# Attention heads: the product with V placed between the sixth and seventh block of a projection

## Chip, cores and metric

One core of a Trainium2 chip runs the whole kernel as one program. The metric is the device time in microseconds (us); the kernel before takes 2199.02 us (median of 3 runs, 2193.82 to 2200.7).

## What is computed

Three transformer layers on 512 positions of width 1024: a retention layer, a layer with chunked attention, and a hybrid layer, each with a feed-forward part. The change lies in the second layer, in its 16 attention heads of width 64:

```python
q, k, v = jnp.split(h @ w_in, 3, axis=-1)            # h: 512 x 1024
s = einsum('bqhd,bkhd->bhqk', qb, kb) * scale + bias # a chunk of 64 queries, a band of up to 576 keys
p = jax.nn.softmax(s, axis=-1)
o = einsum('bhqk,bkhd->bqhd', p, vb)                 # the product with V
return o @ w_out
```

All of it is in fp32. A weight or an activation is split into a high and a low part (`w_hi`, `w_lo`, `x_hi`, `x_lo`), and three matmuls (high by high, high by low, low by high) stand for one.

## The kernel before

The weights come as a stream of 362 units of 512 KB through a ring of four buffers. For each unit SyncE issues the load, ScalarE (ACT) makes the high part (L978), VectorE (DVE) the low part (L1422), three units ahead of use, and TensorE (PE) uses it in a projection (`proj`): eight blocks of three matmuls with 512 columns (L508, L509, L510) that add up in bank 0 or 1 of PSUM. The order of the work on every engine is written out by hand, and semaphores tie the engines together.

The attention heads run as steps s = -1 to 16. In step s, TensorE works for three heads:

- `turn`: it transposes the probabilities of head s-1 into banks 5, 6 and 7 (ten transposes, L729). It waits until GpSimd (POOL) has normalised the probabilities (L2097). The last two transposes write bank 7, and before them it waits on the semaphore `att.o`, which the sum of the head before raises.
- `proj`: the projection of the q or the k tile of a later pair of heads, in steps -1 to 12. Steps 13 to 16 have `two_tiles` in its place: one unit of the output projection, in two halves of 12 matmuls.
- `weigh`: the product with V for head s-1, eight matmuls into bank 7 (L742, L744). It waits for `turned_lo`, the low parts of the transposed probabilities.
- `scores`: q by k for head s+1, eight matmuls (L708, L709), in steps up to 14. It waits for the parts of q and k, and for the `maxima` of head s.

The low part of V lies beside the high part in the stationary operand, so that the halves of bank 7 (64 partitions each) have to be added: ACT copies one half into the pair's tile (`o_part`, L1180), and DVE adds the other (`o_sum`, L1712), which raises `att.o`.

Steps alternate by `head_par`. The text calls a step with `head_par` 0 an even-head step (s = 1, 3, 5, 7, 9, 11, 13, 15) and one with `head_par` 1 an odd-head step (s = 2, 4, ..., 16). The queues of ACT and DVE in a step of the kernel before, in order:

- ACT, even-head: high part of V (`value_hi`, L1195), high parts of the transposed probabilities (`turned_his`, L1164), weight split (L978), four exponentials (L1156), `q_hi` (L1169), two `k_hi` (L1175), `o_part` (L1180).
- ACT, odd-head: the same without L1195; `q_hi` waits here for the q and k tile that DVE reads out of this step's projection (`qk_tile`, L1686), and from step 6 on `out_hi` (L1185) stands between `k_hi` and `o_part`.
- DVE, even-head: `maxima` of head s (L1659, L1663), low part of V (L1730), `turned_los` (L1674), weight split (L1422), `inverse` (L1679), `q_lo` (L1693), `k_lo` (L1700), `qk_tile` (L1686), `o_sum` (L1712).
- DVE, odd-head: the same without L1730, but `qk_tile` stands ahead of `q_lo` and `k_lo`, and `out_lo` (L1719) behind them, ahead of `o_sum`.
- In steps 13 to 16 DVE adds the two halves of `two_tiles` to `h` (L1472) in place of `qk_tile`; only step 13 has `q_hi`, `k_hi`, `q_lo`, `k_lo`, and steps 13 to 15 have `out_hi` and `out_lo`.
- POOL: it adds a mask to the next head's bias (L2110), normalises head s (four instructions, L2097) as soon as `inverse` is done, and loads a bias tile (L2105).

Of the kernel before, what the change touches and what calls it, by code (L numbers as in the profile page):

```python
# [46 lines left out]
HEAD, WINDOW = 64, 128  # L47
# [147 lines left out]
def build(nc, stream, x_t, cols, wf, f_bias, sinks, rel_pad, rel_2, c_rope, c_decay, c_sq, c_tri, c_sel,  # L195
# [3 lines left out]
    with ExitStack() as ctx:  # L199
# [80 lines left out]
        xl_ready = sem("xl_ready")  # L280
# [68 lines left out]
        att = Heads("att")  # L349
# [78 lines left out]
        def pair_tile(pair, a=0, b=P):  # L428

            if not pair.a:  # L430
                return arena[a:b, (9 + pair.b) * S:(10 + pair.b) * S]
            return arena[a:b, bass.ds((pair * S + 9 * S).val(), S)]
# [68 lines left out]
        def _(pe):  # L501
# [16 lines left out]
            def proj(src=xs, n=KT, first=None, hooks={}, bank=None):  # L518


                slot = at.u % RING
                wait(pe, lo_ready, at.u + 1)
                rotating = bank is None
                if rotating:
                    bank = banks[at.t % 2]

                    wait(pe, tile_read, at.t - 1)
                for k in range(n):
                    if k in hooks:
                        hooks[k]()  # L530
                    if first:
                        for s, base in first:
                            wait(pe, s, lin(base) + (k + 1))
                    m = mm3(bank[:, :], w_at(slot, k * P, k * P + P), src(k), k == 0, k == n - 1)
                m.then_inc(products_done, 1)
                at.step(1, 1 if rotating else 0)
# [50 lines left out]
            def two_tiles(src, first=None):  # L587

                slot = at.u % RING
                wait(pe, lo_ready, at.u + 1)  # L590
                for c in range(2):
                    wait(pe, tile_read, at.t - 1)
                    for k in range(4):
                        if first and c == 0:
                            wait(pe, first[0], first[1] + (k + 1))
                        m = mm3(banks[at.t % 2][:, :], w_at(slot, (4 * c + k) * P, (4 * c + k + 1) * P),
                                src(k), k == 0, k == 3)
                    m.then_inc(products_done, 1)
                    at.pe, at.t = at.pe + 1, at.t + 1
                at.u = at.u + 1  # L600
# [132 lines left out]
            def weigh(sm, hd, values, kind):  # L733


                window = kind == "window"
                ta, tw = (CT_AT, CT_W) if window else (T_AT, T_W)
                wait(pe, sm.turned_lo, hd * 4 + 4)
                wait(pe, sm.o, hd)
                for j in range(TT):  # L740
                    dst = banks[7][:, j * P:j * P + tw[j]]
                    pe.matmul(dst, values(j), pt_h[:, ta[j]:ta[j] + tw[j]], start=j == 0, stop=False,  # L742
                              skip_group_check=True)
                    m = pe.matmul(dst, values(j), pt_l[:, ta[j]:ta[j] + tw[j]], start=False, stop=j == TT - 1,  # L744
                                  skip_group_check=True)
                m.then_inc(sm.pv, 1)


            def staged(half):
                return lambda j: vs[:, j, half * P:half * P + P]  # L750
# [4 lines left out]
            def att_step(s, par, unit=True, late=True, early=True, half=None):  # L755


                head_par = par
                if late:
                    turn(att, s - 1, head_par, "chunk")  # L760
                if unit:
                    proj()
                if half is not None:

                    two_tiles(attended, (xl_ready, 24) if half == 0 else None)
                if late:
                    if head_par == 0:

                        wait(pe, stage_lo, (s + 1) // 2)
                    weigh(att, s - 1, staged(head_par), "chunk")  # L770
                if early:

                    wait(pe, att.qk_lo, s * 2 + 4)
                    wait(pe, att.biased, (s + 1) * 4)
                    if s.b == -1:

                        pe.wait_ge(masks_ready, 1)
                        pe.wait_ge(squares_landed, 16)
                        pe.wait_ge(att_v, 8)
                        pe.wait_ge(zeroed, 2)  # L780
                    scores(att, s + 1, head_par, "chunk")
# [178 lines left out]
        def _(act):  # L960
            hold = holder(xh_ready)
# [189 lines left out]
            def exps(sm, hd, par, window=False):  # L1151

                hold(act, (sm.negmax, hd + 1))
                for t in range(TT):
                    a, w = (CP_AT[t], CP_W[t]) if window else (P_AT[t], P_W[t])
                    act.activation(pf[par][:, a:a + w], pf[par][:, a:a + w], ACT.Exp, bias=nm[par][:, t:t + 1],  # L1156
                                   accum_out=sums[par][:, t:t + 1]).then_inc(sm.exp, 1)
# [19 lines left out]
            def o_part(sm, dst, half):  # L1177

                lo = HEAD * half
                act.activation(dst, banks[7][HEAD - lo:2 * HEAD - lo, :], ACT.Copy).then_inc(sm.o_part, 1)  # L1180
# [7 lines left out]
            def att_step(s, head_par, unit=False, late=True, early=True, pair=None, half=False, ended=None,  # L1188
                         sets=True):

                if late:
                    if head_par == 0:

                        hold(act, (att.pv, s - 1))
                        act.activation(value_hi(vs), two_heads(pair_tile(pair)), ACT.Copy).then_inc(stage_hi, 1)  # L1195
                    turned_his(att, s - 1)
                if unit:
                    split()
                    at.step()
                if half:  # L1200
                    split()
                    at.step(2, 2)
                if early:
                    exps(att, s, 1 - head_par)
                if sets:
                    if head_par:
                        wait(act, tile_read, at.t)
                    q_hi(att, 1 - head_par)
                    k_hi(att, 1 - head_par)
                if ended is not None:  # L1210
                    out_hi(ended)
                if late:
                    lo = HEAD * head_par
                    hold(act, (att.pv, s))
                    o_part(att, pair_tile(pair, lo, lo + HEAD), head_par)

            root(2)
            keep_rms(2)
# [186 lines left out]
        def _(dve):  # L1405
# [271 lines left out]
            def inverse(sm, hd, par):  # L1677
                wait(dve, sm.exp, hd * 4 + 4)
                dve.reciprocal(rinv[par], sums[par]).then_inc(sm.rinv, 1)  # L1679
# [41 lines left out]
            def att_step(s, head_par, unit=False, late=True, early=True, pair=None, half=None, ended=None,  # L1721
                         sets=True):

                if early:
                    hd = s
                    maxima(att, hd, 1 - head_par, (bias_masked, hd + 1), "rel")
                if late:
                    if head_par == 0:
                        wait(dve, stage_hi, (s + 1) // 2)
                        dve.tensor_tensor(value_lo(vs), two_heads(pair_tile(pair)), f32(value_hi(vs)),  # L1730
                                          ALU.subtract).then_inc(stage_lo, 1)
                    turned_los(att, s - 1)
                if unit or half is not None:
                    split()
                if early:
                    inverse(att, s, 1 - head_par)
                if sets and not head_par:
                    q_lo(att, 1, s * 3 + 6)
                    k_lo(att, 1, s * 3 + 6)
                if half is not None:  # L1740
                    at.u = at.u + 1
                    for c in range(2):
                        at.pe, at.t = at.pe + 1, at.t + 1
                        add_tile(2 * half + c)
                if unit:
                    at.step()
                    qk_tile(att, head_par, s * 2 + (6 - 2 * head_par))
                if sets and head_par:
                    q_lo(att, 0, s * 3 + 6)
                    k_lo(att, 0, s * 3 + 6)  # L1750
                if ended is not None:
                    out_lo(ended)
                if late:
                    lo = HEAD * head_par
                    hold(dve, (att.o_part, s))
                    o_sum(att, pair_tile(pair, lo, lo + HEAD), head_par)

            def first_pair(sm, n):
                for k in range(2):
# [579 lines left out]
```

## Time and profile before

| | |
|---|---|
| time of the profiled execution | 2198.44 us |
| its span | 2196.7 us |
| TensorE busy | 2127.8 us (97% of the span) |
| VectorE busy | 1239.8 us (56%) |
| ScalarE busy | 850.9 us (39%) |
| GpSimd busy | 270.8 us (12%) |
| mean granted TensorE clock | 0.988 of full speed |

The profile is of one execution. A matmul's row shows its start and its modelled length; matmuls overlap, so a busy TensorE has one 512-column matmul start every 0.23 us while each row says 0.39 us. A view's "idle before" is the time that the engine stood still before an instruction, with what ended it. The attention steps with the product with V lie between 879 and 1037 us of the span.

### The profile page before, as it was taken

How to read it: one execution, taken by the hardware profiler on the slowest of the kernel's cores; microseconds unless marked ns; L12 is line 12 of the kernel's file. 1: busy time of each engine (PE TensorE's matmuls, PEld its weight loads, DVE VectorE, ACT ScalarE, POOL GpSimd, SP SyncE). 2: the span in 40 equal slices, each digit the busy share in tenths (PEclk: the TensorE clock that was granted, in tenths of full speed). 3: DMA queues.
4: the chain of work that ended last, by engine and by line, in shares of the span. 5: the costliest groups of instructions: out<-in, count | busy, mean ns of one | idle time of the engine just before them, and what ended most of it. 6: DMA issues, size and time to landing. Idle time of an engine off the chain costs nothing.

```text
span 2196.7 us, 27184 instructions
## 1 busy us (share of the span) xinstructions
PE 2127.8 (97%) x9700; PEld 1752.2 (80%) x9700; DVE 1239.8 (56%) x1822; ACT 850.9 (39%) x1358; POOL 270.8 (12%) x312
## 2 busy tenths in 40 slices
PE   7899999899999999999999999999999999999997
PEld 5788888788888888777888888867887888888886
DVE  5264646464544543887645445556765456656674
ACT  4243333342222233776422222437662234333342
POOL 4122222310000010332100000302310010000001
PEclk9999999999999999999999999999999999999999
DMA  7532323123333233222333333321223222333332
GB/s 184 113 100 76 101 72 95 57 87 96 96 95 99 93 98 104 77 75 73 92 97 96 95 96 95 101 82 53 73 73 95 94 93 92 106 105 115 96 108 94
DMA packets 58124, 205.51 MB, mean 94 GB/s; under 512 B 7061, under 2 KB 7205, under 8 KB 58048
## 3 DMA queue, kind: packets, MB, share of 16 engines
q1 hardware_dynamic: 52704, 189.82, 27.7%
q0 software_dynamic: 3760, 11.92, 2.9%
q10 hardware_dynamic: 1584, 2.75, 0.3%
q8 instruction: 49, 0.80, 0.1%
q14 instruction: 27, 0.22, 0.0%
HBM read 198.43 MB, written 6.03 MB: 93 GB/s over the span
## 4 chain that ended last, share of the span: by engine, by line
PE 87%; DVE 5%; ACT 3%; issue 2%; POOL 1%; DMA 1%; ACTq 0%; DVEq 0%; POOLq 0%; SPq 0%
PE bank L508 28%; PE bank L510 27%; PE bank L509 27%; DMA raw<-in_stream 1%; PE bank L729 1%; DVE w_lo L1422 1%; POOL arena L2097 1%; ACT w_hi L978 1%; PE bank L744 1%; ACT arena L1156 0%; PE bank L708 0%; PE bank L742 0%; DVE arena_r L1674 0%; DVE h L1472 0%; ACT arena_r L1175 0%
## 5 line engine op out<-in xcount | busy, mean ns | idle before, releaser
L1422 DVE TENSOR_TENSOR w_lo<-raw,w_hi 128x1024 fp32r<-128x1024 f32 x358 | 465.1, 1300 | 288.5 <-ACT w_hi L978 288.5
L508 PE MATMUL bank<-x_hi,w_hi 128*128 128x512 f32 x1552 | 617.9, 398 | 7.3 <-DVE x_lo L1428 4.4
L510 PE MATMUL bank<-x_hi,w_lo 128*128 128x512 f32 x1552 | 607.4, 391 | 0.0
L509 PE MATMUL bank<-x_lo,w_hi 128*128 128x512 f32 x1552 | 607.2, 391 | 0.0
L978 ACT ACTIVATE w_hi<-raw 128x1024 fp32r<-128x1024 f32 x358 | 376.0, 1053 | 417.8 <-PE bank L510 394.0
L508 PE MATMUL bank<-arena_r,w_hi 128*128 128x512 f32 x1008 | 395.2, 392 | 13.6 <-POOL arena_r L2060 7.0
L510 PE MATMUL bank<-arena_r,w_lo 128*128 128x512 f32 x1008 | 393.1, 390 | 0.0
L509 PE MATMUL bank<-arena_r,w_hi 128*128 128x512 f32 x1008 | 393.0, 390 | 0.0
L508 PEld LDWEIGHTS bank<-x_hi,w_hi 128*128 128x128 f32 x1552 | 293.6, 189 | 73.1 <-DVE x_lo L1428 6.3
L509 PEld LDWEIGHTS bank<-x_lo,w_hi 128*128 128x128 f32 x1552 | 293.6, 189 | 62.1 <-issue 3.1
L510 PEld LDWEIGHTS bank<-x_hi,w_lo 128*128 128x128 f32 x1552 | 293.1, 189 | 62.1
L508 PEld LDWEIGHTS bank<-arena_r,w_hi 128*128 128x128 f32 x1008 | 189.6, 188 | 60.2 <-issue 12.1
L1472 DVE TENSOR_TENSOR h<-bank,h 128x512 f32<-128x512 f32 x152 | 104.5, 689 | 224.2 <-PE bank L510 224.0
L510 PEld LDWEIGHTS bank<-arena_r,w_lo 128*128 128x128 f32 x1008 | 189.7, 188 | 39.8
L509 PEld LDWEIGHTS bank<-arena_r,w_hi 128*128 128x128 f32 x1008 | 189.8, 188 | 38.5
L1467 DVE TENSOR_TENSOR arena<-bank,rbc 128x512 f32<-128x512 f32 x125 | 86.3, 690 | 171.7 <-PE bank L510 164.2
L1133 ACT ACTIVATE arena_r<-arena 128x512 fp32r<-128x512 f32 x64 | 40.5, 633 | 247.3 <-DVE arena L1624 247.3
L2033 POOL TENSOR_TENSOR acc<-sq 128x512 f32<-128x512 f32 x6 | 8.3, 1386 | 860.2 <-ACT sq L990 509.1
L2097 POOL TENSOR_SCALAR arena<-arena,small 128x256 f32<-128x256 f32 (+3 forms) x128 | 77.2, 618 | 289.2 <-DVE small L1679 244.9
L508 PE MATMUL bank<-w_hi,x_hi 128*128 128x512 f32 x224 | 87.6, 391 | 0.9 <-ACT arena L1232 0.9
L510 PE MATMUL bank<-w_hi,x_lo 128*128 128x512 f32 x224 | 87.2, 389 | 0.0
L509 PE MATMUL bank<-w_lo,x_hi 128*128 128x512 f32 x224 | 87.2, 389 | 0.0
(215 smaller groups left out, 2012.7 us busy)
## 6 DMA issues: line engine op xcount, KB each, us to landing
raw<-in_stream SPq DMA_DIRECT2D x358, 512.0 KB, 3.5
arena<-in_rel_pad POOLq DMA_DIRECT2D x16, 256.0 KB, 2.9
bias_strips<-arena POOLq DMA_DIRECT2D x1, 3840.0 KB, 55.2
h<-in_x_t ACTq DMA_DIRECT2D x8, 256.0 KB, 6.5
out_t<-h SPq DMA_DIRECT2D x8, 256.0 KB, 2.1
arena<-in_c_decay POOLq DMA_DIRECT2D x4, 256.0 KB, 2.9
arena<-bias_strips POOLq DMA_DIRECT2D x4, 256.0 KB, 3.8
arena<-bias_strips POOLq DMA_DIRECT2D x8, 128.0 KB, 2.4
```

The source lines that it names most:

```text
L508: pe.matmul(dst, lh, rh, start=start, stop=False, **kw)
L509: pe.matmul(dst, lh, rl, start=False, stop=False, **kw)
L510: return pe.matmul(dst, ll, rh, start=False, stop=stop, **kw)
L729: m = pe.transpose(banks[b][:, o + (t - j) * P:o + (t - j) * P + P], pf[par][:, src:src + P], ident[:, :])
L744: m = pe.matmul(dst, values(j), pt_l[:, ta[j]:ta[j] + tw[j]], start=False, stop=j == TT - 1, skip_group_check=True)
L978: act.activation(w_hi[:, u % RING, :], raw[:, u % RING, :], ACT.Copy).then_inc(hi_ready, 1)
L1133: act.activation(uh[j], uf[j % 2], ACT.Copy).then_inc(u_hi, 1)
L1422: dve.tensor_tensor(w_lo[:, s, :], raw[:, s, :], f32(w_hi[:, s, :]), ALU.subtract).then_inc(lo_ready, 1)
L1467: return dve.tensor_tensor(dst, banks[(at.t - 1) % 2][:, :], rbc[:, :], ALU.mult)
L1472: dve.tensor_tensor(h[:, j, :], banks[(at.t - 1) % 2][:, :], h[:, j, :], ALU.add).then_inc(tile_read, 1)
L2033: pool.tensor_tensor(acc[:, :], sq[:, 0, :], sq[:, 1, :], ALU.add).then_inc(acc_sum, 1)
L2097: pool.tensor_scalar(pf[par][:, a:a + w], pf[par][:, a:a + w], rinv[par][:, t:t + 1], 1.0, ALU.mult, ALU.mult).then_inc(sm.probs, 1)
```

## The change

In steps 1 to 12 `weigh` is no longer issued behind the projection but inside it, ahead of its seventh block. ACT's `o_part` goes ahead of `q_hi`, `k_hi` and `out_hi` in all steps 1 to 16. DVE's `o_sum` goes, in steps 1 to 12, directly behind `inverse`, ahead of `q_lo`, `k_lo`, `qk_tile` and `out_lo`; in steps 13 to 16 it stays last. The count and the kinds of the instructions stay the same. The hybrid layer's heads keep their order.

```diff
 # tensor
                 if late:
                     turn(att, s - 1, head_par, "chunk")
-                if unit:
-                    proj()
-                if half is not None:
-
-                    two_tiles(attended, (xl_ready, 24) if half == 0 else None)
-                if late:
+                def weigh_last():
                     if head_par == 0:
 
                         wait(pe, stage_lo, (s + 1) // 2)
                     weigh(att, s - 1, staged(head_par), "chunk")
+
+                if unit:
+                    proj(hooks={6: weigh_last} if late else {})
+                if half is not None:
+
+                    two_tiles(attended, (xl_ready, 24) if half == 0 else None)
+                    weigh_last()
...
 # scalar
                 if early:
                     exps(att, s, 1 - head_par)
+                if late:
+                    lo = HEAD * head_par
+                    hold(act, (att.pv, s))
+                    o_part(att, pair_tile(pair, lo, lo + HEAD), head_par)
                 if sets:
...
                 if ended is not None:
                     out_hi(ended)
-                if late:
-                    lo = HEAD * head_par
-                    hold(act, (att.pv, s))
-                    o_part(att, pair_tile(pair, lo, lo + HEAD), head_par)
...
 # vector
+                def sum_last():
+                    lo = HEAD * head_par
+                    hold(dve, (att.o_part, s))
+                    o_sum(att, pair_tile(pair, lo, lo + HEAD), head_par)
+
...
                 if early:
                     inverse(att, s, 1 - head_par)
+                if late and half is None:
+                    sum_last()
                 if sets and not head_par:
...
                 if ended is not None:
                     out_lo(ended)
-                if late:
-                    lo = HEAD * head_par
-                    hold(dve, (att.o_part, s))
-                    o_sum(att, pair_tile(pair, lo, lo + HEAD), head_par)
+                if late and half is not None:
+                    sum_last()
```

## Rows read from the trace of the kernel before

**Rows 1.** The page: busy us of TensorE, its share of the span, instructions.

```profile
PE 2127.8 (97%) x9700; PEld 1752.2 (80%) x9700; DVE 1239.8 (56%) x1822; ACT 850.9 (39%) x1358; POOL 270.8 (12%) x312
```

**Rows 2.** Waits, 870 to 1040 us: total us, times, longest us.

```profile
PE bank L729 <- DVE arena L1712: 8.8, 7, 1.6
...
PE bank L729 <- POOL arena L2097: 2.1, 2, 1.4
```

**Rows 3.** Busy us by stretch, step 6 and the start of step 7, then on.

```profile
929.90:940.80 10.90, 9.31 (x52) 7.91 (x51) 8.19 (x19) 8.30 (x19) 3.46 (x7) 1.00 0.31 98
940.80:950.20 9.40, 9.33 (x51) 7.84 (x52) 8.44 (x23) 7.01 (x17) 3.52 (x6) 1.00 0.18 57
```

**Rows 4.** Timeline of TensorE, steps 6 and 7: start us, length us.

```profile
929.97 0.48 PE L508 MATMUL bank<-x_hi,w_hi 128*128 128x512 f32 x1
...
935.51 0.39 PE L742 MATMUL bank<-arena_r 128*128 128x512 f32 x1
...
936.72 0.27 PE L708 MATMUL bank<-arena_r 128*128 128x128 f32 x1
...
938.05 1.03 PE L729 MATMUL bank<-ident,arena 128*128 128x128 f32 x8
...
940.67 0.44 PE L729 MATMUL bank<-ident,arena 128*128 128x128 f32 x2 [1.58 <-DVE arena L1712]
...
946.44 0.39 PE L742 MATMUL bank<-arena_r 128*128 128x512 f32 x1
```

**Rows 5.** Timeline of ACT and DVE between step 6 and step 7.

```profile
935.71 0.69 DVE L1686 SCALAR_TENSOR_TENSOR arena<-bank,rbc 128x512 f32<-128x512 f32 x1 [0.56 <-PE bank L510]
...
937.09 1.29 ACT L1175 ACTIVATE arena_r<-arena 64x512 fp32r<-64x512 f32 x2
...
938.28 0.62 ACT L1185 ACTIVATE arena_r<-arena  x1
938.41 0.68 DVE L1700 TENSOR_TENSOR arena_r<-arena,arena_r 64x512 fp32r<-64x512 f32 x1 [0.56 <-ACT arena_r L1175]
938.93 0.59 ACT L1180 ACTIVATE arena<-bank 64x512 f32 x1
939.20 0.69 DVE L1719 TENSOR_TENSOR arena_r<-arena,arena_r  x1
...
939.93 0.69 DVE L1712 TENSOR_TENSOR arena<-bank,arena 64x512 f32 x1
...
940.65 0.29 DVE L1659 CUSTOM_DVE_ANT_0 arena<-bank,arena 128x128 f32<-128x128 f32 x1
...
943.23 1.68 DVE L1674 TENSOR_TENSOR arena_r<-bank,arena_r 128x512 fp32r<-128x512 f32 x4
```

**Rows 6.** Timeline of GpSimd: the normalising of steps 6 and 7.

```profile
935.25 2.06 POOL L2097 TENSOR_SCALAR arena<-arena,small 128x128 f32<-128x128 f32 x4 [2.93 <-DVE small L1679]
...
946.23 2.93 POOL L2097 TENSOR_SCALAR arena<-arena,small 128x128 f32<-128x128 f32 x4 [5.38 <-DVE small L1679]
```

**Rows 7.** Timeline, TensorE's weight loads: the transposes of step 2.

```profile
889.76 1.07 PEld L729 LDWEIGHTS bank<-ident,arena 128*128 128x128 f32 x10 [1.80 <-POOL arena L2097]
```

**Rows 8.** Timeline, steps 13 to 16.

```profile
1006.64 0.63 ACT L1169 ACTIVATE arena_r<-arena 64x512 fp32r<-64x512 f32 x1
...
1007.34 0.39 PE L742 MATMUL bank<-arena_r 128*128 128x512 f32 x1
...
1012.01 0.44 PE L729 MATMUL bank<-ident,arena 128*128 128x128 f32 x2 [0.85 <-DVE arena L1712]
...
1019.79 0.69 DVE L1712 TENSOR_TENSOR arena<-bank,arena 64x512 f32<-64x512 f32 x1 [0.53 <-ACT arena L1180]
...
1020.31 0.93 PE L729 MATMUL bank<-ident,arena 128*128 128x128 f32 x7
...
1028.91 0.68 DVE L1712 TENSOR_TENSOR arena<-bank,arena 64x512 f32<-64x512 f32 x1 [0.54 <-ACT arena L1180]
1028.99 1.31 PE L729 MATMUL bank<-ident,arena 128*128 128x128 f32 x10 [0.74 <-POOL arena L2097]
```

## The prediction

> **What bounds the kernel now.** I read the page first: TensorE is busy for 97% of the span [rows 1], so a change of order can save only where TensorE stands still. The view of waits over the attention steps says how much that is and where: 8.8 us in seven waits for bank 7, which `o_sum` (L1712) has to release, and 2.1 us in two waits for GpSimd's normalising [rows 2]. The stretches show the rhythm: a step from an odd head to the next even head takes 10.90 us with 9.31 us of TensorE in it, the next one 9.40 us with 9.33 [rows 3]. So the wait stands in every second step, ahead of the even heads. The timelines of TensorE and of the two vector engines in steps 6 and 7 then say what is late: TensorE has issued eight transposes at 938.05, and the last two only come at 940.67, 1.58 us late [rows 4]. `o_sum` ended at 940.62, because it stands last in a queue of `qk_tile` 935.71, `k_hi` 937.09, `out_hi` 938.28, `o_part` 938.93, `out_lo` 939.20 and itself 939.93 [rows 5]. `o_part` needed only the product with V, done near 936.9, two us earlier.
>
> **What the change removes.** All times below are in the clock of the trace. A projection takes 935.51 - 929.97 = 5.54 us, so its six first blocks take 4.16 and the last two 1.38. `weigh` takes 936.72 - 935.51 = 1.21, `scores` 938.05 - 936.72 = 1.33 [rows 4]. In step 6 `weigh` would be issued at 934.13 and over at about 935.5. `o_part` (0.59) and `o_sum` (0.69) follow [rows 5] and end at about 936.9; bank 7 is needed at 938.9. So this wait goes, all seven times: 8.8 us of gain if nothing takes its place.
>
> **What takes its place, steps 2 to 12.** Moving `weigh` ahead of two blocks delays the end of the projection by 1.21. `qk_tile` starts at 936.92 instead of 935.71, just behind the moved `o_sum`. From there the old queue runs, without `o_part` and `o_sum`: `qk_tile` to 937.61, `q_hi` to 938.27, the two `k_hi` (1.29) to 939.59, `k_lo` (0.68) to 940.30, `out_lo` (0.69, 0.1 of gap) to 941.06 [rows 5]. `maxima` of step 7 starts at 941.10, before at 940.65: later by 0.45, though a sum has left the queue. Behind `maxima` stand the low part of V and `turned_los`, which before ran from 943.23 to 944.91 [rows 5] and now ends at 945.36.
>
> TensorE, freed of its wait, starts the projection of step 7 at 939.12 and reaches the seventh block at 943.28. There it now meets `weigh`, which needs `turned_los`: it stands still for 2.1 us, inside the projection. Before, `weigh` came at 946.44 [rows 4], 1.5 us after its data, and hid this chain. Now it comes at 945.42, 1.0 us earlier, but 1.38 us of projection still lie behind it. 945.42 + 1.21 + 1.38 + 1.33 = 949.34 is the start of the next transposes; before it was 946.44 + 1.21 + 1.33 = 948.98 and a wait of 0.25 for GpSimd. The next projection starts at 950.41 against 950.28 (929.90 + 10.90 + 9.40 and the same 0.07 [rows 3]): +0.1 per pair of steps. So the removed wait comes back in full, in another place. The first two pairs have no `out_hi` and `out_lo` in the queue; I take 0 for them, and +0.1 for the next three, together +0.3.
>
> GpSimd is the other thing that the next step waits for. `inverse` stands behind the weight split, so its start moves from 946.23 to about 946.68. At 2.93 us, as before, it would end at 949.61 and add 0.3 more per pair, six times 1.6 in all at the worst; at 2.06, as in step 6 [rows 6], it is hidden. The 2.93 is there because `q_lo` and `k_lo` run at the same time. The change puts them behind `o_part`, so that at most `q_lo` meets its last instruction. I take half of the 0.87 and hence no wait. [...]
>
> In step 7 `q_hi` now waits for `o_part`, hence for the product. `k_lo` ends at 950.15, `qk_tile` at 950.84, and `maxima` of step 8 starts 1.0 us later than before; its `turned_los` ends at 954.4. Step 8 reaches its seventh block at 950.41 + 4.16 = 954.57. That hides it by 0.15 us and no more.
>
> **The first steps.** The transposes of step 2 waited 1.80 us for GpSimd [rows 7], so that placing `weigh` earlier gives nothing there; only less contention at GpSimd can, 0 to 0.87. I take -0.5.
>
> **Steps 13 to 16.** TensorE's order is the same, but ACT now puts `o_part` ahead of `q_hi`, `k_hi` and `out_hi`, while DVE still adds last. In step 13 `weigh` comes at about 1006.25 (before 1007.34, [rows 8], less the 1.0 gained by then), `o_part` ends at 1008.3, and `q_hi` starts then instead of at 1006.64 [rows 8]. `k_hi`, `k_lo`, both additions to `h`, `out_lo` and `o_sum` follow, as before in that order: bank 7 comes free at 1013.55, before at 1012.01 [rows 8]. **+1.5 us.** In steps 14 and 15 `out_hi` (0.62) and `out_lo` (0.69) ran before during `two_tiles`; now they stand between `o_part` and `o_sum`, +1.3. In step 14 `o_sum` ended at 1020.48 and bank 7 was needed at 1020.31 + 0.84 = 1021.15 [rows 8]: 0.7 was hidden, **+0.7**. In step 15 it ended at 1029.59 and was needed at 1029.85 [rows 8]: **+1.0**. Step 16 has no `out_hi`; +0.2 for what GpSimd and DVE drag behind. Together +3.4, the largest term of the sum.
>
> **Nothing else moves.** SyncE's loads and ACT's weight splits keep their place and lead of three units; the bias loads follow the normalising within half a microsecond; the hybrid layer is untouched. The clock reads 1.00 in both stretches, with waits of 1.6 us in them [rows 3]; a wait of 2.1 us is near that, and I count no change.
>
> **Sum.** -0.5 + 0.3 + 3.4 = +3.2 us on the profiled execution, 2198.44 to 2201.6. That execution lies 0.6 below the median of the runs, so 2202 for the median: +0.15%, less than what a measurement of this kernel tells from no change (0.3%, 6.6 us).
>
> **Rivals.**
>
> 1. *The gain arrives.* If `turned_los` were done when the seventh block is reached, the 8.8 us would stay and only steps 13 to 16 give back 3.4: 2194, -0.25%; without that loss too, 2190, -0.4%. For it speaks that ACT is idle in parts of the queue and the chain is worked out from single starts. Against it: the gap is 2.1 us, each of the DVE instructions in it is read off, and none of them leaves.
> A variant: TensorE could do the last two blocks during the new wait, 6 x 1.38 = 8.3 us. In the trace its projection did not start while two transposes waited for bank 7, though nothing held it [rows 4]. The Trainium skill, TensorE: Matmul & The Clock Gate, section "The mechanism", says that matmuls are "strict FIFO, no reordering"; by that rule, which speaks against the change, the trace agrees.
> 2. *Slower.* One mechanism: in even-head steps `q_hi` waits for the product, which pushes `qk_tile` and `maxima` of the next step by 1.0. Only 0.15 us hides it. If the queue there is longer than my sum (`k_lo` took 0.92 beside GpSimd, 0.68 alone), odd-head steps wait inside their projection too, and what they lose, the next even-head chain starts later by. The bound is that nothing hides `o_part` and `o_sum`, 0.59 + 0.69 - 0.15 = 1.1 us in each of six pairs: 6.8 + 3.2 = +10, 2209, +0.45%. It decides from 0.6 us per pair, where the whole is over 6.6.
> 3. *No effect.* Another engine ends the wait for bank 7 first (the probabilities of the even heads, say), so that steps 2 to 12 stay and only the tail is lost: 2202. The rows name L1712 seven times; it comes to the same number.
>
> **Chances and range.** My forecast, the waits trade places and the tail loses a little: 0.60. The gain arrives: 0.13, about two thirds of it beyond 0.3%. Slower by the q and k split: 0.20, nearly all beyond. No effect: 0.07. A few hundredths of the forecast's own spread, its terms ranging from -0.9 - 0.3 + 2 = +0.8 to 1.6 + 0.3 + 3.4 + 1.5 = +6.8, lie beyond the bound as well. So faster 0.10, same 0.67, slower 0.23. The likeliest case alone spans 2199 to 2207; the range that takes in part of both rivals is 2194 to 2208.
>
> **What the profile after would show.** Right: the waits of L729 for L1712 are gone in steps 2 to 12; L742 waits about 2 us for L1674 in even-head steps, between two blocks; a pair of steps still takes 20.3 to 20.5 us; L729 waits longer for L1712 in steps 14 to 16 (about 2.3, 0.7 and 1.0). Wrong: L742 waits in odd-head steps too, or hardly at all; pairs shorter than 19.5 or longer than 20.9; GpSimd's four instructions still take 2.9 and end the wait.

## The result, and the profile after

The changed kernel takes 2203.67 us (median of 16 runs) against 2196.94 us before. The two medians lie 6.7 us apart; the ratio that is used from here on, with its interval, is 1.0039 (95%: 1.003 to 1.0048). It is slower by 0.4%, some 8.6 us by that ratio. Two runs stand far outside all others and are left out of the ratios: one of 3094.32 us of the kernel before, and one of 11781.56 us of the last experiment. Its profiled execution took 2203.9 us, with a span of 2202.2 us. Line numbers have moved by two or more: `qk_tile` is L1688, `k_lo` L1702, `out_lo` L1721, `maxima` L1661, `turned_los` L1676, `o_part` L1182, `q_hi` L1171, `o_sum` L1714, the normalising L2104. TensorE's lines are the same.

The page and the waits from 870 to 1045 us, which answer to [rows 1, 2]. A releaser called "issue" means that the view names no other engine's instruction; for L742 it stands in the attention heads where `turned_los` (L1676) ended 0.1 us earlier: its four instructions run from 942.73 to 944.41 below, and `weigh` starts at 944.51.

```profile
PE 2129.0 (97%) x9700; PEld 1753.2 (80%) x9700; DVE 1239.3 (56%) x1822; ACT 849.8 (39%) x1358; POOL 265.1 (12%) x312
...
PE bank L742 <- issue: 9.7, 6, 2.3
...
PE bank L729 <- DVE arena L1714: 4.5, 3, 2.9
...
PE bank L742 <- DVE arena_r L1676: 1.0, 1, 1.0
PE bank L729 <- POOL arena L2104: 1.0, 2, 0.5
```

The 8.8 us of waits for bank 7 are 4.5 us now, all in steps 14 to 16, and `weigh` waits 10.7 us where it did not wait at all. TensorE's timeline in steps 6 and 7, which answers to [rows 4]:

```profile
928.63 0.47 PE L508 MATMUL bank<-x_hi,w_hi 128*128 128x512 f32 x1
...
932.82 0.44 PE L742 MATMUL bank<-arena_r 128*128 128x512 f32 x1
...
934.09 0.44 PE L508 MATMUL bank<-x_hi,w_hi 128*128 128x512 f32 x1
...
935.53 0.22 PE L708 MATMUL bank<-arena_r 128*128 128x128 f32 x1
...
937.83 0.49 PE L508 MATMUL bank<-x_hi,w_hi 128*128 128x512 f32 x1
...
944.51 0.47 PE L742 MATMUL bank<-arena_r 128*128 128x512 f32 x1 [2.30 <-issue]
...
945.88 0.73 PE L508 MATMUL bank<-x_hi,w_hi 128*128 128x512 f32 x1
946.42 0.63 PE L509 MATMUL bank<-x_lo,w_hi 128*128 128x512 f32 x1
...
951.11 0.47 PE L508 MATMUL bank<-x_hi,w_hi 128*128 128x512 f32 x1
```

The transposes go through without a wait, the six blocks of step 7 run from 937.83 on, and then TensorE stands for 2.30 us until `weigh` at 944.51. What comes behind it is new: the matmuls of blocks seven and eight start 0.42 us apart and are 0.63 us long, where all others are 0.23 apart and 0.39 long. The stretches show why; the number behind the engines' columns is the granted clock:

```profile
945.80:950.00 4.20, 4.20 (x16) 3.58 (x16) 2.52 (x4) 2.48 (x4) 2.52 (x5) 0.60 0.64 178
1016.00:1023.40 7.40, 7.40 (x27) 5.96 (x28) 5.21 (x16) 4.53 (x13) 2.06 (x4) 0.77 0.18 61
966.90:972.00 5.10, 5.04 (x33) 4.58 (x33) 3.49 (x6) 2.48 (x4) 2.59 (x5) 1.00 0.47 124
```

For part of the first two stretches TensorE runs at 1.2 instead of 2.4 GHz: from 946.00 to 948.50 and from 1017.50 to 1020.40 the granted clock reads 0.50. Both begin behind a wait, of 2.30 us in step 7 and of 2.92 us in step 14. The third stretch lies behind a wait of 2.33 us in step 9, and there the clock stays whole.

DVE and GpSimd between steps 6 and 7, which answers to [rows 5, 6]:

```profile
935.25 0.69 DVE L1714 TENSOR_TENSOR arena<-bank,arena 64x512 f32 x1 [1.33 <-ACT arena L1182]
935.98 0.69 DVE L1688 SCALAR_TENSOR_TENSOR arena<-bank,rbc 128x512 f32<-128x512 f32 x1
...
938.68 0.68 DVE L1702 TENSOR_TENSOR arena_r<-arena,arena_r 64x512 fp32r<-64x512 f32 x1 [0.62 <-ACT arena_r L1177]
...
939.46 0.78 DVE L1721 TENSOR_TENSOR arena_r<-arena,arena_r  x1
...
940.16 0.28 DVE L1661 CUSTOM_DVE_ANT_0 arena<-bank,arena 128x128 f32<-128x128 f32 x1
...
942.73 1.68 DVE L1676 TENSOR_TENSOR arena_r<-bank,arena_r 128x512 fp32r<-128x512 f32 x4
...
945.73 2.05 POOL L2104 TENSOR_SCALAR arena<-arena,small 128x128 f32<-128x128 f32 x4 [6.05 <-DVE small L1681]
```

The chain is the one that the prediction laid out. `o_sum` now ends only as `qk_tile` starts, `qk_tile` starts 7.35 us after the projection's start (935.98 - 928.63) where it was 5.74, `maxima` 11.53 where it was 10.68. GpSimd takes 2.05 us instead of 2.93. Steps 13 to 15, which answers to [rows 8]:

```profile
1010.14 0.60 ACT L1182 ACTIVATE arena<-bank 64x512 f32<-64x512 f32 x1 [1.45 <-PE bank L744]
1010.77 0.63 ACT L1171 ACTIVATE arena_r<-arena 64x512 fp32r<-64x512 f32 x1
...
1015.26 0.68 DVE L1714 TENSOR_TENSOR arena<-bank,arena 64x512 f32<-64x512 f32 x1
...
1015.99 0.44 PE L729 MATMUL bank<-ident,arena 128*128 128x128 f32 x2 [2.92 <-DVE arena L1714]
...
1018.28 0.63 PE L509 MATMUL bank<-arena_r,w_hi 128*128 128x512 f32 x1
...
1024.79 0.59 ACT L1182 ACTIVATE arena<-bank 64x512 f32<-64x512 f32 x1 [3.80 <-PE bank L744]
1025.41 0.63 ACT L1187 ACTIVATE arena_r<-arena 128x512 fp32r<-128x512 f32 x1
...
1026.80 0.69 DVE L1714 TENSOR_TENSOR arena<-bank,arena 64x512 f32<-64x512 f32 x1
...
1027.55 0.44 PE L729 MATMUL bank<-ident,arena 128*128 128x128 f32 x2 [0.58 <-DVE arena L1714]
```

`q_hi` of step 13 follows `o_part`; bank 7 comes free 2.92 us late, then the matmuls of step 14 run slow for some 3 us. In step 14 `out_hi` (1025.41) stands between `o_part` and `o_sum`, and 0.58 us is lost.

The stage can be measured within one trace: from the first matmul of step 1's projection to that of step 16's `two_tiles`. The first two lines are of the kernel before, the last two of the changed kernel:

```profile
880.15 0.48 PE L508 MATMUL bank<-x_hi,w_hi 128*128 128x512 f32 x1
...
1030.05 0.47 PE L508 MATMUL bank<-arena_r,w_hi 128*128 128x512 f32 x1
```

```profile
878.75 0.48 PE L508 MATMUL bank<-x_hi,w_hi 128*128 128x512 f32 x1
...
1037.36 0.48 PE L508 MATMUL bank<-arena_r,w_hi 128*128 128x512 f32 x1
```

Before, this is 149.90 us, after 158.61 us. So the stage is 8.7 us longer. The two spans, 2196.7 and 2202.2 us, differ by 5.5 us only: ahead of step 1 and behind step 16 the execution before took 1.4 and 1.8 us more. These two parts vary among the twelve profiled kernels as well (878.45 to 880.57 us, and 1163.3 to 1166.7 us), and the clock may have a share in it: from 1400 to 1500 us the mean granted clock is 0.95 in the execution before and 0.98 in the one after. This is why kernels are compared here by the stage and not by the span. By step, where the rows are rounded:

| from the projection's start in | before | after | change | predicted |
|---|---|---|---|---|
| step 1 to 2 | 10.68 | 10.37 | -0.3 | -0.5 |
| 2 to 4, 4 to 6 | 39.14 | 39.51 | +0.4 | 0 |
| 6 to 8 (slow clock after) | 20.31 | 22.48 | +2.2 | +0.1 |
| 8 to 10, 10 to 12 | 40.64 | 41.79 | +1.2 | +0.2 |
| 12 to 14 | 21.29 | 23.28 | +2.0 | +1.5 |
| 14 to 15 (slow clock after) | 9.11 | 11.56 | +2.5 | +0.7 |
| 15 to 16 | 8.73 | 9.62 | +0.9 | +1.2 |

### The profile page after: what moved, and what is told of

It is laid out like the page before. It is cut to its first block, busy times and chain, and to the rows that moved or that the text cites. A ratio compares the mean times of both kernels' runs of the same rounds, so it can differ in the third digit from the quotient of the medians.

```text
span 2202.2 us, 27184 instructions
## 1 busy us (share of the span) xinstructions
PE 2129.0 (97%) x9700; PEld 1753.2 (80%) x9700; DVE 1239.3 (56%) x1822; ACT 849.8 (39%) x1358; POOL 265.1 (12%) x312
## 4 chain that ended last, share of the span: by engine, by line
PE 89%; DVE 4%; ACT 3%; issue 2%; DMA 1%; POOL 0%; ACTq 0%; DVEq 0%; POOLq 0%; SPq 0%
PE bank L508 28%; PE bank L509 28%; PE bank L510 28%; DMA raw<-in_stream 1%; PE bank L729 1%; DVE w_lo L1424 1%; PE bank L742 1%; PE bank L744 1%; ACT w_hi L980 1%; PE bank L708 1%; PE bank L709 1%; DVE h L1474 0%; ACT arena_r L1177 0%; PE bank L574 0%; PE bank L562 0%
## 5 line engine op out<-in xcount | busy, mean ns | idle before, releaser
L2104 POOL TENSOR_SCALAR arena<-arena,small 128x256 f32<-128x256 f32 (+3 forms) x128 | 69.8, 559 | 301.1 <-DVE small L1681 256.8
```

The lines of the kernel that those rows point to most:

```text
L2104: pool.tensor_scalar(pf[par][:, a:a + w], pf[par][:, a:a + w], rinv[par][:, t:t + 1], 1.0, ALU.mult, ALU.mult).then_inc(sm.probs, 1)
```

## Experiments

Every kernel was timed against the kernel before on its chip. The chip was not the same for all experiments, so that ratios and not times compare two experiments, and each profile is of one execution. "The stage" is the length from step 1 to step 16 in its own profile, 149.90 us before; "a pair" is the time from the start of step 8's projection to that of step 10's, or of step 10's to that of step 12's.

### Steps 13 to 16 in the old order

```diff
-                if late:                      # scalar: o_part ahead of q_hi, k_hi, out_hi
+                if late and not half:
                     ...
+                if late and not (not half):   # scalar: o_part last
+                    ...
```

> The changed kernel, but in steps 13 to 16 ACT's o_part is last again, as in the kernel before. Theory (the order of ACT in steps 13 to 16 costs most): of the 8.7 us that the changed kernel lost between step 1 and step 16, 5.3 lay from step 12's projection to step 16's; they go, but for about 0.5. Left are +3 to +4 us against before, +0.15%. Rival (the product inside the projection costs most, by waits and by a slower TensorE clock behind them): +7 us or more stay, +0.3%.

Measured: 2199.45 us, ratio 1.002 (1.0009 to 1.0031); the stage 153.44 us, +3.5. The expectation of the theory holds. Of its 3.5 us, one slow stretch is 1.6: it came in step 9 this time, behind a wait of 2.37 us, while steps 7 and 11 had waits of 2.33 and 2.29 and kept the clock.

```profile
966.29 0.47 PE L742 MATMUL bank<-arena_r 128*128 128x512 f32 x1 [2.37 <-issue]
...
967.66 0.74 PE L508 MATMUL bank<-x_hi,w_hi 128*128 128x512 f32 x1
968.20 0.63 PE L509 MATMUL bank<-x_lo,w_hi 128*128 128x512 f32 x1
```

### Steps 13 to 16 alone

```diff
 # the kernel before, scalar
                 if early:
                     exps(att, s, 1 - head_par)
+                if late and half:
+                    ...                       # o_part
                 if sets:
                     ...
-                if late:
+                if late and not half:
```

> The kernel before, with ACT's o_part ahead of q_hi, k_hi and out_hi in steps 13 to 16 alone. Theory: +3.2 us by the working of the prediction, and up to 1.7 more if the wait for bank 7 in step 14 (0.85 + 1.7 = 2.5 us) is followed by a stretch at half the clock, as in the changed kernel: +3 to +5 us, +0.15 to 0.23%. Rival (these steps only pass on what the steps before them lost): 0.

Measured: 2202.53 us, ratio 1.0023 (1.0014 to 1.0032), +5 us, at the upper end of what was expected; the stage 155.77 us, +5.9, is above it. So one move on ACT, in four steps that have no product inside a projection, costs more than half as much as the whole change. (The +3.5 of the last experiment and these +5.9 add up to more than 8.7: the move costs less, 5.2 us, on top of the rest of the change.) The wait for bank 7 in step 14 is 3.67 us, where 2.5 was expected, with a slow stretch behind it:

```profile
1014.94 0.44 PE L729 MATMUL bank<-ident,arena 128*128 128x128 f32 x2 [3.67 <-DVE arena L1716]
...
1016.52 0.63 PE L510 MATMUL bank<-arena_r,w_lo 128*128 128x512 f32 x1
```

### Even-head steps alone, odd-head steps alone

```diff
-                    proj(hooks={6: weigh_last} if late else {})
+                    proj(hooks={6: weigh_last} if late and head_par == 0 else {})   # or == 1
...
-                if late and half is None:                    # vector: the sum behind inverse
+                if late and half is None and head_par == 0:  # or == 1
```

ACT's `o_part` goes with them, and steps 13 to 16 are as before in both.

> Weigh inside the projection, o_part early and o_sum early in even-head steps alone; odd-head steps and steps 13 to 16 as before. Theory (the chain from the odd-head projection's end over qk_tile, q_hi, k_hi, out_lo, maxima, turned_los sets the pace): the chain starts as before, the wait for bank 7 of 1.6 us comes back, the wait inside the projection is under 0.2 us, GpSimd takes 2.1 instead of 2.9 us and the wait for it goes: -0.2 to -0.3 us per pair, -1 to -2 us in all. Rival (any product inside a projection costs, clock or restart): +1 us or more.

> Weigh inside the projection, o_part early and o_sum early in odd-head steps alone; even-head steps and steps 13 to 16 as before. Theory: no wait for bank 7, but the chain starts 1.6 us later and is 0.8 us later at maxima; GpSimd still takes 2.9 us beside q_lo and k_lo and now ends the wait: +0.8 us per pair, +4 to +5.5 us, +0.2 to 0.25%. Rival (the wait for bank 7 was time lost, and only the even-head steps' order gives it back): -4 us or better.

Even heads alone: 2197.23 us, ratio 1.0003 (0.9994 to 1.0012), the stage 148.41 us, -1.5. Odd heads alone: 2198.07 us, ratio 1.001 (1.0002 to 1.0019), the stage 153.66 us, +3.8. The first two lines are of the even-head kernel, the last two of the odd-head kernel:

```profile
943.88 2.05 POOL L2109 TENSOR_SCALAR arena<-arena,small 128x128 f32<-128x128 f32 x4 [5.23 <-DVE small L1686]
...
958.36 0.44 PE L729 MATMUL bank<-ident,arena 128*128 128x128 f32 x2 [1.54 <-DVE arena L1719]
```

```profile
947.25 0.47 PE L742 MATMUL bank<-arena_r 128*128 128x512 f32 x1 [0.96 <-issue]
...
951.53 1.31 PE L729 MATMUL bank<-ident,arena 128*128 128x128 f32 x10 [1.49 <-POOL arena L2109]
```

With even heads alone GpSimd takes 2.05 us, nothing waits for it, the wait for bank 7 stays at 1.54, and a pair takes 20.08 us, 0.3 less than before. The trace bears the theory out; the run times can't tell it from no change. With odd heads alone the wait for bank 7 is gone, and two others stand in its place, 0.96 for `turned_los` and 1.49 for GpSimd: a pair takes 21.2 us, 0.8 more than before. The stage lost a little less than expected, because the first pairs, without `out_hi`, lost 0.5; by the run times the loss is some 2 us (0.4 to 4.2). So, as the traces show it, the harm is in the odd-head steps, whose projection ends later, and not in a product inside a projection as such.

### TensorE kept at work in its waits

```diff
+            def fill(n, bank, read):
+                if n:
+                    wait(pe, tile_read, read)
+                for _ in range(n):
+                    pe.matmul(bank[:, 0:256], x_hi[:, 0, 0:P], x_hi[:, 0, 0:256],
+                              start=True, stop=True, skip_group_check=True)
...
                 def weigh_last():
+                    if head_par == 0 and unit:
+                        fill(8, banks[(at.t - 1) % 2], at.t)
```

and `fill(12, ...)` in the transposes of step 14, ahead of the wait for bank 7.

> The changed kernel, and in its longer waits TensorE works instead of standing still: eight spare matmuls of 256 columns (some 0.9 us) ahead of weigh in every even-head step, and twelve (1.4 us) ahead of the wait for bank 7 in step 14. Their results are read by nobody. Theory (a wait of over 2 us is at times followed by a stretch at 1.2 GHz, which cost 1.4 us in step 7 and 1.7 us in step 14 of the changed kernel's profile): no wait is longer than 1.5 us, no stretch of matmuls at 0.43 us spacing follows, and the kernel with 68 more matmuls is about 3 us faster than the changed one: +5 to +6 us against before, +0.25%. Rival (the slow stretches have another cause): they stay, +0.4% or more.

Measured: 2201.9 us, ratio 1.0029 (1.0018 to 1.004); the stage 155.48 us, +5.6, against +8.7 of the changed kernel. No matmul of the stage is slow, and every pair from step 6 on takes 20.9 us. The two lines are the `weigh` of step 7 and the filling of step 14:

```profile
945.96 0.47 PE L750 MATMUL bank<-arena_r 128*128 128x512 f32 x1 [1.41 <-issue]
...
1014.18 1.69 PE L720 MATMUL bank<-x_hi 128*128 128x256 f32 x12 [1.13 <-DVE h L1484]
```

The kernel has 60 matmuls more (the expectation miscounted them) and its stage is shorter: the remaining 3.1 us of the changed kernel were the clock, 1.6 in step 7 and 1.7 in step 14, less 0.1 elsewhere. (As ratios the two lie 0.1% apart, and their intervals overlap; the stage in the traces is the sharper reading, of one execution each. In steps 7, 9 and 11 the full clock could also be chance, since two of three such waits were harmless without filling; in step 14 both traces with the moved `o_part` and no filling, of the changed kernel and of steps 13 to 16 alone, have a slow stretch.) What is left, +5.6 us, is the order of the queues. Runs at the same mean granted clock say the same: at 0.989, this kernel took 2201.0 to 2202.5 us and the kernel before on the same chip 2195.6 to 2196.4 us (four runs each), 5.5 us apart in the mean.

### The sum behind the tile

In odd-head steps `sum_last()` stands behind `qk_tile` instead of behind `inverse`; steps 13 to 16 are in the old order.

> The changed kernel with steps 13 to 16 in the old order, and DVE's o_sum in odd-head steps behind qk_tile instead of ahead of it. Theory (the part of the slower pairs that the prediction missed is o_sum, which ends after the projection and holds qk_tile up): qk_tile starts 0.2 to 0.3 us earlier in the step, and so does everything to turned_los; pairs of steps 6 to 12 take 20.6 instead of 20.9 us; against before +1 to +3 us with up to 1.4 for a slow stretch, +0.1%. Rival (the lost time is in the restart of TensorE after its wait): pairs stay at 20.9.

Measured: 2199.44 us, ratio 1.0023 (1.0012 to 1.0035); the stage 153.49 us. The forecast of 20.6 us per pair failed. `qk_tile` did start 0.25 us earlier in the step (7.10 instead of 7.35), but `maxima` only 0.07 (11.46 instead of 11.53), and pairs took 20.8 and 21.0 us as without it. The timeline shows where the rest went: `out_lo` (L1725) still starts 0.26 us earlier (10.57 instead of 10.83), but from its start to `maxima` it takes 0.89 us instead of 0.70. It now runs wholly beside GpSimd's addition of the mask (L2123), in step 6 as in steps 8, 10 and 12, where the same stretch takes 0.83 to 1.01 instead of 0.71 to 0.72; that this is the cause was not tested.

```profile
936.82 0.69 DVE L1692 SCALAR_TENSOR_TENSOR arena<-bank,rbc 128x512 f32<-128x512 f32 x1 [1.80 <-PE bank L510]
...
940.14 0.46 POOL L2123 TENSOR_TENSOR arena<-arena,sqr 128x128 f32<-128x128 f32 x1 [2.43 <-DMA arena<-in_rel_pad]
940.29 0.85 DVE L1725 TENSOR_TENSOR arena_r<-arena,arena_r  x1
...
941.18 0.29 DVE L1665 CUSTOM_DVE_ANT_0 arena<-bank,arena 128x128 f32<-128x128 f32 x1
...
945.54 0.47 PE L742 MATMUL bank<-arena_r 128*128 128x512 f32 x1 [2.27 <-issue]
```

### out_hi and out_lo out of the chain

```diff
 # scalar, behind the exponentials          # vector, behind inverse
+                if ended is not None and unit:
+                    out_hi(ended)           # out_lo(ended)
...
-                if ended is not None:
+                if ended is not None and not unit:
```

Once in the changed kernel (with the old steps 13 to 16), once in the kernel before.

> The changed kernel with steps 13 to 16 in the old order, and in steps 6 to 12 out_hi and out_lo placed ahead of the sum, where ACT and DVE stand idle for the product, instead of behind k_hi and k_lo. Theory (the chain behind qk_tile sets the pace): 0.8 us leave the chain; the wait inside the projection falls from 2.3 to about 1.5 us, a pair of steps takes 20.1 instead of 20.9 us, no slow stretch follows: from step 1 to 16 1 to 2.5 us shorter than before, -0.05 to -0.1%. Rival (a wait on TensorE or GpSimd takes its place): pairs stay at 20.9, +0.2% as without it.

> The kernel before, with only out_hi and out_lo moved in steps 6 to 12: directly behind the exponentials and behind inverse. Theory (the same chain, ending at GpSimd and the transposes, sets the pace of the kernel before too, and its wait for bank 7 has no price of its own): pairs of steps take 19.6 instead of 20.3 us, as steps 2 to 5, which have no out_hi, do; -2.5 us, -0.12%. Rival: 0, because the wait for bank 7 is the price and o_sum's place in the queue stays.

In the changed kernel: 2195.68 us, ratio 0.9999 (0.999 to 1.0008); the stage 148.48 us, -1.4; pairs 20.13 and 20.07 us instead of 20.9, waits inside the projection 1.44 to 1.53 us, no slow stretch. By the trace the theory holds: what leaves the chain leaves the pair; the run times alone can't tell this kernel from the one before. The `weigh` of step 7:

```profile
943.89 0.47 PE L742 MATMUL bank<-arena_r 128*128 128x512 f32 x1 [1.44 <-issue]
```

In the kernel before: 2195.84 us, ratio 1.0002 (0.9993 to 1.0011), the stage 150.45 us, pairs 20.5 us instead of 20.3. The expectation failed. There the exponentials end just before the projection does, so that `out_lo` is not covered and pushes `qk_tile` back by what it saves behind it:

```profile
934.51 0.62 ACT L1185 ACTIVATE arena_r<-arena  x1
...
935.43 0.87 DVE L1721 TENSOR_TENSOR arena_r<-arena,arena_r  x1 [0.61 <-ACT arena_r L1185]
936.22 0.68 DVE L1688 SCALAR_TENSOR_TENSOR arena<-bank,rbc 128x512 f32<-128x512 f32 x1
...
940.46 0.44 PE L729 MATMUL bank<-ident,arena 128*128 128x128 f32 x2 [1.72 <-DVE arena L1714]
```

`qk_tile` starts 6.60 us after the projection's start (929.62), before 5.74. So this run did not test whether the wait for bank 7 has a price.

### A shorter chain

Even-head steps as changed; odd-head steps with the product behind the projection; in odd-head steps

```diff
                     q_hi(att, 1 - head_par)
+                    ...                       # o_part
                     k_hi(att, 1 - head_par)
...
                     q_lo(att, 0, s * 3 + 6)
+                    if late and half is None:
+                        sum_last()
                     k_lo(att, 0, s * 3 + 6)
```

and in step 13 `o_sum` ahead of the additions to `h`.

> Even-head steps in the changed order, odd-head steps with the product behind the projection as before, out_hi and out_lo early, and o_part between q_hi and k_hi, o_sum between q_lo and k_lo, where DVE waits for ACT; in step 13 o_sum ahead of the additions to h; in steps 14 to 16 as before. Theory: the chain does not start later (qk_tile does not wait for the product), bank 7 is free by 8.6 us after the odd-head projection's start and is needed at 9.0, the wait inside the even-head projection is 0.6 us: pairs of steps take about 19.0 us, and the stage from step 1 to 16 is 6 us or more shorter than before: -0.25 to -0.35%. Rival (GpSimd or ACT has become the bound): pairs of 19.6 or more, -0.15% or less.

Measured: 2192.08 us, ratio 0.9986 (0.9977 to 0.9995); the stage 145.41 us, -4.5. It is the first kernel that beats the one before, but by half of what was expected: pairs take 19.7 us from step 6 on, and 19.0 and 19.1 only in the first two, which have no `out_hi`. These are the numbers of the expectation's rival, but not for its reason: as in the last experiment, `out_lo` stands in the way of `qk_tile`. The last kernel moves it to the even-head steps, where ACT and DVE wait for the product:

```diff
-                             ended=Lin(j // 2, 2, i) if j % 2 else None)
+                             ended=None if j % 2 else Lin(j // 2, 2, i))
```

> As the kernel with the short chain, but out_hi and out_lo stand in even-head steps, behind the exponentials and inverse, where ACT and DVE wait 1.6 us for the product. Theory (out_lo ahead of qk_tile held that one up by 0.7 us in odd-head steps): qk_tile starts 5.7 us after the odd-head projection instead of 6.4, the wait for bank 7 of 0.2 us and 0.3 of the wait inside the projection go, pairs of steps 6 to 12 take 19.0 us as the first two pairs instead of 19.7: the stage from step 1 to 16 is 6.5 us shorter than before, -0.25%. Rival: the even-head steps pay it back at qk_tile and maxima, pairs stay at 19.7, -0.14%.

Measured: 2189.9 us, ratio 0.9977 (0.9967 to 0.9986); the stage 143.04 us, -6.9. Pairs take 19.1 us, no wait for bank 7 is left, and from step 7 on the wait inside the even-head projection is 0.55 to 0.59 us, as the theory had it:

```profile
941.20 0.47 PE L742 MATMUL bank<-arena_r 128*128 128x512 f32 x1 [0.55 <-issue]
...
960.28 0.47 PE L742 MATMUL bank<-arena_r 128*128 128x512 f32 x1 [0.59 <-issue]
```

This kernel beats both, the one before by 0.23% and the changed one by some 0.6% (0.9977 against 1.0039; these two were not timed side by side).

## Why the prediction came out as it did

**Range and sign: the sign right, the size too small, the hit partly luck.** 2202 was forecast, 2203.67 measured, inside 2194 to 2208. Part of that closeness is luck: the forecast started from 2199.02, the median of three runs before, and over all sixteen that kernel came out at 2196.94. The loss itself was forecast at 3.2 us and came out at 8.6 by the ratio (6.7 by the two medians). The likeliest case was "within 0.3%" at 0.67, and the ratio came out at +0.39%, in a class that had been given 0.23, and for other reasons than the ones that this chance stood for.

**The exchange of waits: right.** The wait for bank 7 left steps 2 to 12, and the wait for `turned_los` took its place between blocks six and seven, 2.30 us where 2.1 was worked out. TensorE did not do blocks seven and eight in the meantime. The even-head and odd-head runs show that the chain through `qk_tile` sets the pace, and the two runs that take work out of it show pairs shorter by 0.6 to 0.8 us.

**GpSimd: right.** 2.05 us instead of 2.93, and no wait for it in steps 8 to 12. Even-head steps alone, where `o_part` also precedes `q_hi`, show the same 2.05.

**Pairs of steps: mis-sized.** "I take 0 for them, and +0.1 for the next three" measured +0.2 for each of the first two and +0.6 for each of the next three, the slow stretch left out. At 20.9 us a pair stands on the forecast's own bound for being wrong ("longer than 20.9"). Of the 0.4 at `maxima` (11.53 against 11.13 worked out), 0.15 is the projection with the product in it, 6.90 us instead of 6.75. The other 0.25 is `o_sum`, which ends after the projection and holds `qk_tile` up; the forecast had it end at about 936.9, just in time. With it moved away every instruction up to `out_lo` came 0.25 earlier, but `out_lo` took 0.2 longer, so that only 0.07 came back at `maxima`.

**Steps 13 to 16: right in kind, right in size without the clock.** +3.4 was forecast; with the waits filled the trace shows +3.7 from step 12 to step 16 (2.0, 0.8, 0.9), of which 0.2 is left when these steps have the old order. Single waits were 2.92, 0.58 and 1.01 us, forecast about 2.3, 0.7 and 1.0. Moving ACT's `o_part` there alone cost +5.9 with its slow stretch, some 4.2 without: in the kernel before the same move costs more than in the changed one.

**The clock: the step that failed.** "A wait of 2.1 us is near that, and I count no change." The profile after has two slow stretches, worth 3.1 us of the 8.7. Without them 5.6 us are left, 0.25%, and the run with the waits filled came out at +0.29%: it took both, the clock and the mis-sized pairs, to get past 0.3%. The argument went from waits of 1.6 us to one of 2.1, and missed that the forecast itself put the wait of step 14 at 0.85 + 1.5 = 2.4 us or more.

**The slower rival** named odd-head waits. In steps 6, 10 and 12 the weight load ahead of `weigh` waits 0.2 us, which delays the matmuls by less than 0.1; in step 8 nothing waits. This is as small as the 0.15 of cover suggested, and did not decide.

## What to carry to other kernels

A wait that one engine shows can be the slack of a longer chain over the others: before it is removed, follow what releases it once around the loop, and see what the next wait is and whether it grows. Moving work ahead of a projection's end delays whatever reads that projection; here the chain of reads was the bound and not TensorE. An instruction that waits for a late result belongs behind those that don't (`o_part` behind `q_hi`, `out_hi` ahead of `o_part`), and a place is free only if the engine stands idle there in that kernel: the same move of `out_lo` gained 0.8 us per pair in one kernel and nothing in the other.

## What the runs showed of the hardware

TensorE's clock halved behind long waits, but not behind each of them (the granted clock is 0.50 in the slow stretches of the changed kernel, one half of full speed). In the attention heads of the traces, none of the waits of 1.72 us or less was followed by slow matmuls; of nine waits between 2.25 and 2.39 us (in the changed kernel and two of the experiments) three were; both of 2.92 and 3.67 us were. A slow stretch made six or seven 512-column matmuls start 0.43 us apart instead of 0.23, and cost 1.5 to 1.7 us (a step of 13.28 us where the others like it took 11.73). The step in which it fell differed between kernels with the same waits (7, 9 and 7). The sixteen runs of the changed kernel go with the mean granted clock of the run: 2200.0 and 2201.1 us at 0.990, 2207.1 to 2209.1 at 0.985.

GpSimd's four instructions of the normalising took 2.05 us in step 6 of the changed kernel, where neither `q_lo` nor `k_lo` ran beside them, and 2.93 us in step 7 of the kernel before, where both did. There `q_lo` and `k_lo` took 0.78 and 0.92 us, in step 6 of the changed kernel 0.69 and 0.68.
